# Three staging slots for streamed weights and five places for their split halves, instead of four and four

## What is computed

```python
def hybrid_layer(x, ...):                     # twice
    proj = rms_norm(x, norm1_g) @ w_in         # 1024 x about 8200
    ... gated linear attention, block attention, mLSTM on slices of proj ...
    mixed = (gates[:, :, 0] * (y_gla @ w_br_gla) + gates[:, :, 1] * (y_moba @ w_br_moba)
             + gates[:, :, 2] * (y_mlstm @ w_br_mlstm))
    x = x + mixed @ w_out
    return x + jnp.square(jax.nn.relu(rms_norm(x, norm2_g) @ w_ff1)) @ w_ff2

def hierarchical_moe(h, ...):                  # in the second block, 32 experts in 4 groups of 8
    ... a group for each token, then two experts of the group, with weights `combine` ...
    for e in range(N_EXPERTS):
        hid = jax.nn.silu(t @ w_gate[e]) * (t @ w_up[e])
        out = out + combine[:, e:e + 1] * (hid @ w_down[e])
```

## Time and profile before

| | us |
|---|---|
| median of 3 runs | 1839.73 (1835.38 to 1841.78) |
| the profiled execution | 1837.81 |
| its span | 1835.9 |
| PE busy | 1601.8 (87% of the span) |
| DVE busy | 1171.0 (64%) |
| ACT busy | 866.9 (47%) |
| POOL busy | 140.2 (8%) |

### The profile page before, as it was taken

The page is one execution under the profiler, slowest core; times in us unless marked ns, Lnnn a source line. Parts: engine busy times, 40 slices in busy tenths (PEclk is TensorE's granted clock), DMA queues, the critical chain, the costliest instruction groups (busy, mean ns, idle before and its releaser), DMA issues.

```text
span 1835.9 us, 19829 instructions
## 1 busy us (share of the span) xinstructions
PE 1601.8 (87%) x7216; PEld 1294.8 (71%) x7216; DVE 1171.0 (64%) x1521; ACT 866.9 (47%) x1130; POOL 140.2 (8%) x133
## 2 busy tenths in 40 slices
PE   5999776979998899976897999788697799999995
PEld 4887555768887788754676888666576688877774
DVE  4666544757777566653474777754555655689996
ACT  4535532444443543542334444434443344577773
POOL 0074000000000018200000000000000000000000
PEclk9999788989999899976798999979898799999998
DMA  6444212456766354310245677542220545599992
GB/s 266 161 162 154 74 46 71 159 196 238 266 257 223 126 185 159 140 67 23 92 143 191 255 272 265 216 184 92 92 93 4 191 172 175 206 350 353 357 351 77
DMA packets 45440, 326.06 MB, mean 178 GB/s; under 512 B 5280, under 2 KB 5280, under 8 KB 6688
## 3 DMA queue, kind: packets, MB, share of 16 engines
q1 hardware_dynamic: 38304, 278.94, 42.1%
q0 software_dynamic: 4608, 33.56, 4.7%
q10 hardware_dynamic: 2432, 12.30, 1.8%
HBM read 323.73 MB, written 1.05 MB: 177 GB/s over the span
## 4 chain that ended last, share of the span: by engine, by line
PE 54%; issue 31%; DVE 9%; ACT 6%; DMA 1%; POOL 0%; POOLq 0%; ACTq 0%; DVEq 0%; SPq 0%
PE PS L148 50%; PE PS L153 3%; ACT w_hi L162 2%; ACT S L162 2%; DVE PR L169 1%; DVE w_lo L169 1%; DVE G L169 1%; DVE S L180 1%; DVE PR L180 1%; DVE st L188 1%; DVE MS L169 1%; DVE S L169 0%; ACT L162 0%; DVE S L200 0%; DVE X L169 0%
## 5 line engine op out<-in xcount | busy, mean ns | idle before, releaser
L169 DVE TENSOR_TENSOR w_lo<-stage,w_hi 128x1024 fp32r<-128x1024 f32 x532 | 656.4, 1239 | 470.8 <-ACT w_hi L162 463.9
L162 ACT ACTIVATE w_hi<-stage 128x1024 fp32r<-128x1024 f32 x532 | 561.4, 1060 | 643.2 <-PE PS L148 634.3
L148 PE MATMUL PS<-w_hi,a_hi 128*128 128x512 f32 x1168 | 487.8, 418 | 33.1 <-DVE G L169 18.6
L148 PE MATMUL PS<-w_lo,a_hi 128*128 128x512 f32 x1168 | 472.2, 404 | 0.0
L148 PE MATMUL PS<-w_hi,a_lo 128*128 128x512 f32 x1168 | 470.9, 403 | 0.0
L148 PEld LDWEIGHTS PS<-w_hi,a_hi 128*128 128x128 f32 x1168 | 230.1, 197 | 93.2 <-DVE G L169 20.8
L148 PEld LDWEIGHTS PS<-w_hi,a_lo 128*128 128x128 f32 x1168 | 229.3, 196 | 50.8
L148 PEld LDWEIGHTS PS<-w_lo,a_hi 128*128 128x128 f32 x1168 | 230.4, 197 | 46.0 <-issue 1.2
L148 PE MATMUL PS<-w_hi,h_hi 128*128 128x512 f32 (+1 forms) x480 | 192.7, 401 | 9.7 <-issue 6.0
L148 PE MATMUL PS<-w_hi,h_lo 128*128 128x512 f32 (+1 forms) x480 | 188.1, 392 | 0.0
L148 PE MATMUL PS<-w_lo,h_hi 128*128 128x512 f32 (+1 forms) x480 | 188.0, 392 | 0.0
(11 more groups left out here) (204 smaller groups left out, 1400.1 us busy)
## 6 DMA issues: line engine op xcount, KB each, us to landing
stage<-wall SPq DMA_DIRECT2D x170, 1024.0 KB, 4.9
stage<-wexp SPq DMA_DIRECT2D x96, 1024.0 KB, 5.0
PR<-wada POOLq DMA_DIRECT2D x32, 1024.0 KB, 7.6
G<-gate_b ACTq DMA_DIRECT2D x2, 1536.0 KB, 7.3
PR<-rows ACTq DMA_DIRECT2D x1, 2048.0 KB, 10.7
lsm<-small ACTq DMA_DIRECT2D x3, 563.0 KB, 3.6
X<-x_in ACTq DMA_DIRECT2D x1, 1024.0 KB, 5.1
PR<-rows ACTq DMA_DIRECT2D x1, 1024.0 KB, 5.6
```

Source lines behind the costliest of these rows:

```text
L148: ins = self.e.matmul(out, lhsT, rhs, start=start, stop=stop, skip_group_check=True)
L162: self.tell(self.e.activation(out, in_, func, **kw), sem, chain)
L169: self.tell(self.e.tensor_tensor(out, a, b, op), sem, chain)
```

## The change

`STAGES` goes from 4 to 3 and `SPLITS` from 4 to 5. A slot of `stage` and a pair of places in `w_hi` and `w_lo` both hold 8 KB in each partition, so the memory in use stays the same. The two loops that issue the first splits of the experts now run five times, with four sorting steps as before.

```diff
-STAGES = 4
-SPLITS = 4
+STAGES = 3
+SPLITS = 5
@@ SIGNALS
-landed0 landed1 landed2 landed3
+landed0 landed1 landed2
@@ experts_act
             for b in range(SPLITS):
-                sort_first_act(a, b)
+                if b < KD // 2:
+                    sort_first_act(a, b)
                 split_hi(a, DENSE_HALVES + b)
@@ experts_dve
             for b in range(SPLITS):
-                sort_first_dve(v, b)
+                if b < KD // 2:
+                    sort_first_dve(v, b)
                 split_lo(v, DENSE_HALVES + b)
             weights_dve(v)
             spent_dve(v, 4)
```

## The result

Twelve runs of the kernel after have a median of 1849.23 us (1837.76 to 1860.65), twelve of the kernel before beside them 1839.18 us (1834.68 to 1842.63). The ratio is 1.0058, with an interval of 1.0037 to 1.0080: **the change makes the kernel 0.58% longer, by some 10 us** (7 to 15). The forecast was +6 us, the range reached to 1856.

The account below looks back on a forecast made before the run. PE was taken to bound the dense parts, with everything tight in the one-tile experts. Terms +2 + 3.5 + 1.5 + 1.2 - 1.8 - 0.3 = +6.1 us; against the median, 1839.7 + 6 = 1845.8 us, range 1839 to 1856.

Parts of the forecast that it names:

- the side given the higher chance: Whole kernel: slower by over 0.3%, chance 0.50, against 0.45 for within 0.3%.
- The place: Dense stretches cost nothing and their windows stay; the ring's loss falls in the one-tile experts.
- The mechanism: One-tile experts: position 3's slot loop closes on itself, late units delay the SiLU and PE's product; +2 us.
- The start: Start of the kernel: the fifth split needs the third unit and delays the first norm; +1.5 us.
- The routing: Ahead of the routing weights: one more remainder moves the chain that PE waits for; +1.2 us.
- The fifth place: Layers 0 and 1: PE's waits for a remainder go, -1.8 us; `w_lo` waits fall from four to one or two.
- The rounds and the disturbed transfers: One-tile experts: about 0.1 us a round, +2 us; late transfers at group starts and disturbed stretches, +3.5 us (0 to 8).
- The ring becomes the bound: Rival, one-tile experts: transfers of 5.3 us make the round 9.35, about 1853 us; chance 0.22.
- The ring fits: Rival, one-tile experts: transfers stay at 4.8 us, idle time absorbs disturbances, total 1841.5 us; chance 0.28.
- faster: Rival: the fifth place removes PE's waits for halves and before the 24 transposes, 1827 us; chance 0.05.

Follow-up runs that it names:

- e3: The changed kernel with only the first half of each expert transfer fetched, all instructions kept; median 1837.4 us, ratio 1.0001 to the kernel before.
- e8: The kernel before with the experts' SiLU and the product behind it moved ahead of the split behind position 3; 1827.62 us, 0.65% less than before.
- e9: The changed kernel with splits running four halves ahead in the experts instead of five; median 1838.9 us, ratio 1.0015 to the kernel before.
- e1: The kernel before with three staging slots instead of four, still four places; 1841.16 us, ratio 1.0015 to the kernel before.
- e5: The changed kernel with its staging memory as six half slots, each filled by its own 0.5 MB transfer; 1847.64 us, ratio 1.0060 to the kernel before.

## Why the prediction came out as it did

The time came out in the range and on the side given the higher chance; even the lower end of the interval, +0.37%, is past the 0.3%. At an equal clock the change costs 13.7 us (error 1.3), more than twice the +6; that the median came nearer to the forecast than the profile and this estimate did is then luck. By its steps:

- **The place.** Right. The whole difference of the profiles lies in the one-tile stretch; the dense window has PE at 46.00 of 46 us, and ACT waits there for no DMA.
- **The mechanism.** Right in the main, and shown by e3: the slot's loop closes on itself, its transfer comes onto the path, and PE pays at the product behind the SiLU (1.6 to 14.9 us). The waits lie at positions 3 and 5, as the prediction named them; 34 against "some 20 at least". It took the 0.5 us at position 5 for hidden and closed the loop for position 3 alone; the loop of position 5 closes as well and is the longer one.
- **The start.** +1.6 us measured, +1.5 forecast.
- **The routing.** +0.8 us measured, +1.2 forecast. PE's long wait there is 3.5 us as before.
- **The fifth place.** PE's waits for `w_lo` fell from four to one of 0.3 us, as forecast. Whether the 1.8 us were gained can't be told. The mixer parts of the two layers took 369.3 and 381.5 us before, 374.6 and 374.4 after, but e8, whose layers are those of before, has 379.9 and 372.2, and the granted clock of a stretch such as 230 to 275 us was 0.85 in one profile and 0.71 in the other. A gain of 1 or 2 us is lost in that. The 2.1 us that the start and the routing had cost and that are gone at 1600 us are no proof of it either: ahead of the stretch the mean clock was 0.917 after and 0.915 before, which at 13.0 us for 0.01 is worth as much.
- **The rounds and the disturbed transfers: mis-sized.** +2 and +3.5 were forecast, 13.0 was measured in the profile. The larger part of the error is in the second term: the six rounds at the group starts and in the disturbed stretch cost 8.7 us, above the 8 that the prediction gave as its upper end. The three rounds behind the group starts lost 1.8, 1.9 and 1.6 us, the top of its "nothing to 2 us". It counted on ACT's idle time to take the larger part; in fact the short rounds in which the engines had caught up are gone. The first term is 4.3 us over the other 17 rounds, 0.25 a round. Its own sum gave 0.04 to 0.09 and took the upper end. The 4.85 to 4.9 us for a transfer came from three of the fastest: in the one-tile stretch the median was 5.0 after and 5.1 before, the mean 5.2 and 5.7. *Disturbed* was treated as the exception, when 36 of 64 transfers before, and 30 of 65 after, took over 5.0 us.
- **The rivals.** "The ring becomes the bound" had the round at 9.35 and 1853 us. (Its sum gives +11 and 2.7 for start and routing, 13.7; the "+12" there is a slip.) In the profile this is nearer the truth (9.44, +13.3) than the forecast itself; in the medians the result lies between the two. "The ring fits" is out, and so is "faster". What "the ring becomes the bound" said of a transfer of 5.3 us is in the round shown above; its reason, gaps for want of waiting transfers, wasn't separated from plain variation.
- **What the prediction didn't see.** It worked out positions, but not that the parity of the lead decides what stands between the two halves of a unit. With the same three slots a lead of four loses 0.5 (e9) to 4.4 us (e1) of stretch and one of five 13.0. e1 and e9 have the same order in the tail, but not the same places: in e9 ACT may split when PE has finished the half five back, in e1 four back. So the 4 us between them can be what the fifth place gives where it doesn't disturb the pairing, or the chance of single profiles; at an equal clock they are 2.2 us apart (error 1.6).

Open: four slots with five places, which would say what the fifth place does by itself, would need another 8 KB in each partition and weren't tried. What sets the granted clock of a run, and with it most of the 23 us between the runs after, no run isolates.

## What to carry over

Count the budget of a ring in the stage that turns it fastest, from the spread of its transfer times there and not from the quickest, and see which operations stand between the two halves of one buffer: they lengthen its hold. Look also at the irregular rounds: the reserve that let this kernel catch up behind each group was worth more than that of the even rounds. A ring that came out at zero reserve on paper lost here, since transfers vary. And where an engine's split may wait, look at what is queued behind it: moving one SiLU ahead of one split gained more (0.65%) than either division of the memory. Where times of one kernel differ by more than the effect looked for, hold them against the granted clock of the runs first.

## What the runs showed of the hardware

- A transfer of 1 MB landed 4.7 us after its issue at the quickest (before and after), one of 0.5 MB after 3.5 us (e3, one-tile stretch): half of the bytes took off 1.2 us.
- Transfers took longer where more were waiting and more was moved; the two aren't separated. 0.5 MB took 6.0 us with six slots (e5, 347 GB/s) and 4.4 with three (e3), and 1 MB 7.0 us in e8, where DMA moved 365 GB/s over 150 us.
- Waits for DMA have no fixed price in this kernel. ACT's 34.4 us of them in e9 came with a stretch 0.5 us longer than before, its 31.0 us after with one 13.0 us longer. What counted was what reached PE: 5.4 us of waits for the product in e9, 14.9 after.
- A run's mean granted clock and its time went together: 13.0 us for 0.01 of full speed over 191 runs of kernels of this form, at clocks from 0.912 to 0.933.
